# Attention of a two-layer encoder: key bands of 23 and 31 columns in place of 24 and 32, and a new order of half turns, token turns and one score product on TensorE

## The reference, cut to what matters

```
q, k, v = split(rms_norm(x) @ w_in)            # 8 heads of 64, on a 16 x 64 grid
for each query at (row, col):
    row0 = clip(row - 4, 0, 8);  col0 = clip(col - 8, 0, 48)
    keys = grid[row0 : row0+8, col0 : col0+16]                 # 8 x 16 = 128 keys
    p    = softmax(q . k[keys] / 8 + rpb[h, drow, dcol])
    out  = p @ v[keys]
mix = head_rms_norm(concat[out, gmlp(z), fourier(xc)]);   x = x + mix @ w_out
x = x + swiglu(rms_norm(x))
```

## Time and profile before

| | |
|---|---|
| median of 3 runs | 2007.32 us (2007.18 to 2007.69) |
| the profiled execution | 2007.3 us, span 2005.5 us |
| busy: PE, PEld, DVE, ACT, POOL | 99%, 82%, 76%, 45%, 11% of the span |
| granted PE clock | 1.0 (mean 0.999) |
| attention, layer 1 and 2 | about 199 to 290 us and 1190 to 1290 us of the span |
| DMA | 288.91 MB, mean 144 GB/s; 227.77 MB read from and 59.24 MB written to HBM |

### The profile page before, as it was taken

The page is one execution under the profiler, slowest core; times in us unless marked ns, Lnnn a source line. Parts: engine busy times, 40 slices in busy tenths (PEclk is TensorE's granted clock), DMA queues, the critical chain, the costliest instruction groups (busy, mean ns, idle before and its releaser), DMA issues.

```text
span 2005.5 us, 28816 instructions
## 1 busy us (share of the span) xinstructions
PE 1981.8 (99%) x10528; PEld 1647.2 (82%) x10528; DVE 1530.2 (76%) x2511; ACT 895.3 (45%) x1611; POOL 221.0 (11%) x156
## 2 busy tenths in 40 slices
PE   8999999999999999999999999999999999999998
PEld 7887788888888888888898877888888888888887
DVE  8847874799777777787777488567997777778877
ACT  7453873443333333444544549535333333344443
POOL 1221453100000000000013123630000000000000
PEclk9999999999999999999999999999999999999999
DMA  7965743124432338533477668331343233293333
GB/s 247 214 168 154 228 156 119 43 99 170 132 110 90 106 109 288 174 98 96 120 220 193 156 159 245 138 105 58 129 157 118 90 106 110 100 342 99 95 100 122
DMA packets 130988, 288.91 MB, mean 144 GB/s; under 512 B 12960, under 2 KB 17952, under 8 KB 130592
## 3 DMA queue, kind: packets, MB, share of 16 engines
q1 hardware_dynamic: 107584, 241.97, 37.0%
q0 software_dynamic: 10880, 20.97, 6.3%
q10 hardware_dynamic: 12384, 24.12, 3.4%
HBM read 227.77 MB, written 59.24 MB: 143 GB/s over the span
## 4 chain that ended last, share of the span: by engine, by line
PE 89%; DVE 6%; issue 2%; ACT 2%; DMA 0%; DVEq 0%; SPq 0%; ACTq 0%
PE bank L2249 27%; PE bank L2251 27%; PE bank L2250 27%; PE bank L2470 1%; PE bank L2398 1%; PE bank L2547 1%; DVE s_lo L1484 1%; DVE t_lo L1913 0%; PE bank L2492 0%; PE bank L2361 0%; PE bank L2485 0%; ACT logits L1189 0%; PE bank L2377 0%; DVE logits L1772 0%; DVE att_sq L1829 0%
## 5 line engine op out<-in xcount | busy, mean ns | idle before, releaser
L2249 PE MATMUL bank<-t_hi,s_hi 128*128 128x512 f32 (+1 forms) x1336 | 516.9, 387 | 0.8 <-DVE hid_cu L2026 0.5
L2250 PE MATMUL bank<-t_lo,s_hi 128*128 128x512 f32 (+1 forms) x1336 | 516.3, 386 | 0.0
L2251 PE MATMUL bank<-t_hi,s_lo 128*128 128x512 f32 (+1 forms) x1336 | 516.3, 386 | 0.0
L2249 PEld LDWEIGHTS bank<-t_hi,s_hi 128*128 128x128 f32 x1336 | 250.9, 188 | 52.4 <-DVE hid_cu L2026 1.3
L2251 PEld LDWEIGHTS bank<-t_hi,s_lo 128*128 128x128 f32 x1336 | 250.9, 188 | 50.9
L2250 PEld LDWEIGHTS bank<-t_lo,s_hi 128*128 128x128 f32 x1336 | 251.0, 188 | 50.7
L2249 PE MATMUL bank<-b_hi,s_hi 128*128 128x512 f32 x528 | 206.0, 390 | 0.1
L2251 PE MATMUL bank<-b_hi,s_lo 128*128 128x512 f32 x528 | 205.5, 389 | 0.0
L2250 PE MATMUL bank<-b_lo,s_hi 128*128 128x512 f32 x528 | 205.4, 389 | 0.0
L992 ACT ACTIVATE s_hi<-w_u 128x512 fp32r<-128x512 f32 x142 | 89.6, 631 | 233.1 <-PE bank L2251 175.6
L992 ACT ACTIVATE s_hi<-w_down 128x512 fp32r<-128x512 f32 x154 | 97.3, 632 | 201.9 <-PE bank L2251 199.9
(11 more groups left out here) (296 smaller groups left out, 3704.8 us busy)
## 6 DMA issues: line engine op xcount, KB each, us to landing
w_raw<-in_win SPq DMA_DIRECT2D x51, 512.0 KB, 5.8
w_g<-in_wg SPq DMA_DIRECT2D x44, 512.0 KB, 3.6
w_u<-in_wu SPq DMA_DIRECT2D x44, 512.0 KB, 4.5
t_raw<-hidden_t SPq DMA_DIRECT2D x88, 256.0 KB, 2.6
w_raw<-in_win POOLq DMA_DIRECT2D x40, 512.0 KB, 7.1
t_raw<-hidden_b SPq DMA_DIRECT2D x66, 256.0 KB, 2.6
hidden_b<-hid_g SPq DMA_DIRECT2D x60, 256.0 KB, 2.0
hidden_t<-hid_x SPq DMA_DIRECT2D x44, 256.0 KB, 2.0
```

The lines of the kernel that those rows point to most:

```text
L2249: nc.tensor.matmul(bank, lh, rh, start=start, stop=False, skip_group_check=reopened)
L2250: nc.tensor.matmul(bank, lh, rl, start=False, stop=False, skip_group_check=reopened)
L2251: return nc.tensor.matmul(bank, ll, rh, start=False, stop=stop, skip_group_check=reopened)
```

## The change

`KC` becomes 23, 31, 31, 24; a new `KS` keeps 24, 32, 32, 24 for the score products. So scores are computed as before, and the last column of each row of keys in blocks 0 to 2 is dropped when `logits` reads the bank. All that follows uses `KC`: `L`, the bias tables (laid out on the host with fewer columns), the exponentials, the half turns (chunks of 92 or 124 keys), the value band's partitions and the DMAs that fill them. `BAND` stays 0, 8, 24, 40.

In the odd periods 5, 7, 9, 11 and 13 `turn_tokens` is replaced: each of its four turns is cut into two of 64 rows, and these eight, the twelve half turns of turn_halves(2m) and the two first products of scores(2m+2) are put into one interleaved order, in which instructions of array rows 0 to 63 and 64 to 127 mostly alternate. `ot_full` now counts 2 a tile. Period 15 keeps the old form.

```diff
-KC = [24, 32, 32, 24]
+KC = [23, 31, 31, 24]
+KS = [24, 32, 32, 24]
+NTURN = NCHUNK * P
...
         def score_bank(i, e):
-            return B[e + 4 * (i >= SINGLE and i % 2)][:, 0:keys(i // 4)]
+            j, rr = TILES[i // 4]
+            bank = B[e + 4 * (i >= SINGLE and i % 2)]
+            return bank[:, 0:KR[rr] * KS[j]].rearrange("p (r c) -> p r c", c=KS[j])
...
-                sp.wait_ge(ot_full, l * 8 + 8)
+                sp.wait_ge(ot_full, 2 * (l * 8 + 8))
...
-                    act.wait_ge(ot_full, l * 8 + tile + 1)
+                    act.wait_ge(ot_full, 2 * (l * 8 + tile + 1))
...
+                    def by_row(ap):
+                        return ap.rearrange("p (r c) -> p r c", c=KC[TILES[tile][0]])
                     nc.vector.tensor_tensor_reduce(
-                        L[:, t % 4, 0:keys(tile)], score_bank(t // 2, t % 2),
-                        BIAS[BIAS_BUF[tile]][:, h // 4, h % 4 * keys(tile):(h % 4 + 1) * keys(tile)], -1.0, 3e38,
+                        by_row(L[:, t % 4, 0:keys(tile)]), score_bank(t // 2, t % 2)[:, :, 0:KC[TILES[tile][0]]],
+                        by_row(BIAS[BIAS_BUF[tile]][:, h // 4, h % 4 * keys(tile):(h % 4 + 1) * keys(tile)]), -1.0, 3e38,
...
+                def score(i, n, e):
...
+                    mm = nc.tensor.matmul(
+                        score_bank(i, e), qs[hp, c, q0:q0 + P],
+                        grid(ks[hp, c, :])[:, 4 * rr:4 * rr + KR[rr], BAND[j]:BAND[j] + KS[j]],
+                        start=n == 0, stop=n == 2)
...
+                def half_tokens(tile, k, e):
+                    rows = slice(e * DH, (e + 1) * DH)
+                    mm = nc.tensor.transpose(B[TILE_BANK[tile]][:, k * P + e * DH:k * P + (e + 1) * DH],
+                                             head_squares(tile)[rows, k, :], IDENT[rows, rows])
+                    if k == NP - 1:
+                        mm.then_inc(ot_full, 1)
...
+                def turn_halves_and_tokens(i, tile, following):
+                    before = 2 * (l * 8 + tile)
+                    pe.wait_ge(o_norm, l * 8 + tile + 1)
+                    half_tokens(tile, 0, 1)
+                    pe.wait_ge(pt_dve, l * 32 + i)
+                    pe.wait_ge(pt_act, l * 32 + i)
+                    pe.wait_ge(p_made, l * 64 + 2 * i + 1)
+                    for g in range(3):
+                        half_turn(i, g, 0)
+                        half_tokens(tile, g + 1, 1)
+                    pe.wait_ge(p_made, l * 64 + 2 * i + 2)
+                    half_turn(i, 3, 0)
+                    half_turn(i, 0, 1)
+                    half_turn(i, 4, 0)
+                    half_turn(i, 1, 1)
+                    half_turn(i, 5, 0)
+                    half_turn(i, 2, 1)
+                    scores_ready(following)
+                    score(following, 0, 0)
+                    half_turn(i, 3, 1)
+                    half_turn(i, 4, 1)
+                    pe.wait_ge(ot_full, before + 1)
+                    half_tokens(tile, 0, 0)
+                    half_turn(i, 5, 1)
+                    half_tokens(tile, 1, 0)
+                    score(following, 0, 1)
+                    half_tokens(tile, 2, 0)
+                    half_tokens(tile, 3, 0)
...
-                    scores(2 * m)
+                    if m % 2 or m == SINGLE // 2:
+                        scores(2 * m)
+                    else:
+                        score_terms(2 * m, 1)
...
-                    if m % 2:
-                        turn_tokens((m - 5) // 2)
-                    turn_halves(2 * m)
+                    if m % 2 == 0:
+                        turn_halves(2 * m)
+                    elif m < 15:
+                        turn_halves_and_tokens(2 * m, (m - 5) // 2, 2 * m + 2)
+                    else:
+                        turn_tokens(5)
+                        turn_halves(2 * m)
```

More of the change, by code:

```diff
@@ L275, in build @@
         PT = nc.alloc_sbuf_tensor_at("probs_t", [P, 4 * NCHUNK, P], F32, offset=BASE + shared)
-        small[0] = shared + 4 * NKEY * 4
+        small[0] = shared + 4 * NTURN * 4
         for n, name in enumerate(("cu", "u4u", "t4")):
@@ L2393, in scores, with score_terms @@
                         pe.wait_ge(qk_lo, l * 16 + 8 + i + 1)
+                def score(i, n, e):
+                    tile, c = divmod(i, 4)
+                    j, rr = TILES[tile]
                     q0 = (2 * j + rr) * P
-                    for n, (qs, ks) in enumerate(((QH, KH_), (QH, KL), (QL, KH_))):
-                        for e in range(2):
[L2397 to L2403, removed]
+                    hp = slice(DH * e, DH * e + DH)
+                    qs, ks = ((QH, KH_), (QH, KL), (QL, KH_))[n]
+                    mm = nc.tensor.matmul(
+                        score_bank(i, e), qs[hp, c, q0:q0 + P],
+                        grid(ks[hp, c, :])[:, 4 * rr:4 * rr + KR[rr], BAND[j]:BAND[j] + KS[j]],
+                        start=n == 0, stop=n == 2)
+                    if n == 2:
+                        mm.then_inc(s_full, 1)
+                def score_terms(i, first):
+                    for n in range(first, 3):
+                        for e in range(2):
+                            score(i, n, e)
+                def scores(i):
+                    scores_ready(i)
+                    score_terms(i, 0)
                 for k in range(4):
@@ L2475, in values, with heads_ready @@
                                 mm.then_inc(pv_done, 1)
-                def turn_heads(tile):
+                def heads_ready(tile):
                     pe.wait_ge(o_copied, l * 8 + tile + 1)
@@ L2483, in turn_heads @@
                         pe.wait_ge(bt_lo, l * 8 + 8)
+                def turn_heads(tile):
+                    heads_ready(tile)
                     for k in range(NP):
@@ L2540, in turn_halves @@
                     pe.wait_ge(pt_act, l * 32 + i)
[L2541 to L2548, removed]
-                                    L[rows, t % 4, chunk(t // 8, n)], IDENT[rows, rows])
-                                if s == 1 and n == NCHUNK - 1:
-                                    mm.then_inc(pt_full, 1)
+                    for g in range(2 * NCHUNK):
+                        if g % NCHUNK == 0:
+                            pe.wait_ge(p_made, l * 64 + 2 * i + g // NCHUNK + 1)
+                        half_turn(i, g, 0)
+                        half_turn(i, g, 1)
+                def turn_halves_and_tokens(i, tile, following):
[6 more added lines that the diff above has]
+                    for g in range(3):
+                        half_turn(i, g, 0)
+                        half_tokens(tile, g + 1, 1)
[17 more added lines that the diff above has]
+                    half_tokens(tile, 3, 0)
                 last_half_bank(2, (0, 1))
```

22 lines of the change are left out of this document (14 added, 8 removed).

## The result

The kernel after takes **2205.26 us** (median of 4 runs, 2204.11 to 2205.34), the kernel before 2007.39 us (4 runs, 2007.18 to 2007.69): a ratio of 1.0984, 95% interval 1.0967 to 1.1001. The forecast was 2198 us, in a range of 2172 to 2340. The profiled execution took 2205.23 us, span 2203.4, mean granted clock 0.952.

A forecast was written before the change was run, and what follows sets the result against it. PE, busy 99%, bounds the whole program, but in attention a DVE and ACT ring sets a tile's 8.70 us. Sum: 2007.3 - 0.9 (columns) - 0.4 (order) + 185.6 (DMA stalls) + 6 (clock) = 2198 us, range 2172 to 2340.

The forecast's parts named there:

- Item 4: Value band DMAs of 23 or 31 partitions fall to one engine at 24.2 GB/s; six stalls, 185.6 us.
- Equal parts: Dealing rule for DMAs: the largest number of engines up to 16 dividing the partitions; rounding up was the alternative.
- Slow single engine: Rival: a band load moves only 15.0 GB/s an engine whatever its company; 2338 us in all; chance 0.13.
- (a): Stall of values(0) for block 0's band on one engine: 23.1 us, in layer 2 23.7.
- (b): Stall of values(8) for block 1's band, its loads shifted with values(0): 28.5 us a layer.
- (c): Stall of values(16) for block 2's band, queued behind bias halves, w_out and x_res: 40.9 us a layer.
- Item 5: PE's clock at half speed after each of six stalls: 1 us each, 6 us lost, ends 0 and 12.
- Item 3: New order in five odd periods a layer: 0.38 us saved on PE each, only 0.4 us gained in all.
- the ring: Loop setting a tile's 8.70 us: head_norms, logits on DVE, ACT's exponentials to squares, head_sums on DVE; PE waits inside it.
- PE's order decides: Rival: spread loads with PE setting the pace in the odd periods, 0.38 us x 10 gained; 2002.6 us; chance 0.03.
- Item 1: Narrower logits (12 to 13 ns less on DVE) and exponentials (9 to 10 on ACT): 0.9 us gained in both layers.
- Spread loads: Rival: band loads still use many engines, so only small gains remain; 2006.0 us, ends 2002 and 2012; chance 0.10.

The follow-up runs named there:

- e10: Kernel before, value band loads cut into 21 + 3, 25 + 7 and 22 + 10 partitions, block 3 whole: 2031.18 us, ratio 1.0117.
- e1: Kernel after, each value band load issued as two, partitions 0 to 15 and the rest: 2010.46 us, ratio 1.0016 to before.
- e6: Kernel after, loads of 23 and 31 partitions kept, the reload of x issued behind block 2's loads: 2188.76 us, ratio 1.0903 to before.
- e5: Kernel after, block 0's 23-partition loads left whole, those of blocks 1 and 2 cut into 16 + 15: 2057.26 us, ratio 1.0252 to before.
- e3: Kernel before with only the new order of the odd periods, key columns kept at 24, 32, 32, 24: 2008.25 us, ratio 1.0003.
- e9: Kernel before with the new order alone, and the reload of x behind block 2's loads: 2008.82 us, ratio 1.0005.
- e7: Kernel after, band loads cut in two (16 and the rest), reload of x behind block 2's loads: 2007.17 us, ratio 0.9999 to before.
- e4: Dropped columns alone, in the old order of PE, band loads cut into 16 and the rest: 2010.25 us, ratio 1.0013 to before.

## Why the prediction was right

**Item 4, the DMAs.** The two steps that carried the forecast held. Equal parts: one engine at 23 and 31 (share 0.07), seven at 21. The choice itself had less behind it than the prediction says. The row that it names, the missing time to landing, can't part the two ways of dealing: 24 partitions lie on 12 engines by either, and in the trace of before the 24-partition loads leave 13 landing events and the 32-partition loads 16, with both kinds on each semaphore. So from the rows alone the choice was open. The rate: block 0's four loads landed at 207.1, 215.2, 222.5 and 231.0, some 8.0 us for 188,416 bytes, 23.7 GB/s against the 24.2 taken. "Slow single engine" is excluded by the rate. The 15.0 and 11.6 GB/s an engine of the earlier trace rows fit a limit of the sum, and e10 agrees, where seven engines moved 152 to 160 GB/s, some 22 each; the 104 GB/s of e1's small pieces do not fit it and stay unexplained.

The sizes, a layer each (forecast; layer 1, layer 2):

| wait | forecast | measured |
|---|---|---|
| (a) values(0) | 23.1, 23.7 | 23.2, 22.6 |
| (b) values(8) | 28.5, 28.5 | 29.3, 33.0 |
| (c) values(16) | 40.9, 40.9 | 39.35, 39.8 |
| sum of six | 185.6 | 187.2 |

(a) fits to 1.1 us. Of its terms only the 1.65 us to the first data had no row; the trace of after has 1.2 there, and 31.4 us for the four loads instead of 31.1.

(b) and (c) fit partly by luck. A wait for a band ends when the band lands, so the thing to compare is the time from one value product to the next block's landing:

| from, to | forecast | layer 1 | layer 2 |
|---|---|---|---|
| values(0), block 1 landed | 50.3 | 55.0 | 55.9 |
| values(8), block 2 landed | 58.2 | 58.1 | 57.9 |

The first row is the term that the prediction mis-sized, by some 5 us a layer. I had the transfers on the one engine follow each other at a full rate from fixed issue times. In fact SP was held up in its issues: block 1's loads came 6.2 us after values(0) instead of 4.8, and their data came later still, so that they met x_res. While x_res moved (from 274 us on in layer 1), block 1's fourth load took 15.2 and 16.2 us instead of 10 (from the landing before it to its own). In layer 1 the wait was near its forecast even so, only because PE, at the low clock, came to values(8) 4.1 us late itself: one error hid the other. In layer 2 PE was 1.3 us late, and the wait shows the excess.

The second row is right to 0.3 us, but by two errors that cancel: the first of block 2's loads began some 14.3 us after values(8) instead of 16.2, and the fourth took 13.7 instead of 10. (c) is shorter than its forecast because PE came to values(16) 1.6 and 1.0 us late.

e6 shows what x_res adds. Without it ahead, block 2 lands 50.7 and 50.0 us after values(8), which is 7.4 and 7.9 less, and block 1 lands 52.0 and 52.9 us after values(0), 3.0 and 3.1 less. That the wait for block 1 fell by only 0.1 in layer 1 is again PE, which came 2.9 us sooner.

**Item 5, the clock.** The direction was right, the sum was not. Behind the waits the windows show 0.50, half speed, and then a rise. The earlier trace rows gave 3.3 us at half speed. In after it was some 4.5 us behind the third wait (0.50 from 345 to 348, then 0.81 over 4 us, which is 1.5 us more), and some 12.5 us behind the first (0.50 from 231 to 241, then 0.66 over 4 us, 2.7 us more).

What it cost PE, against before: from values(0) to values(8) 25.98 - 21.84 = 4.1 us in layer 1 and 23.15 - 21.84 = 1.3 in layer 2 (waits left out); from (8) to (16) 1.6 and 1.0; from (16) to values(30) 1.4 and 1.0. But only the last pair adds to the time. The others lie ahead of a wait for a band, and shorten it by as much, unless the band's loads start later for them. They do not: block 1's loads were issued 6.2 us after values(0) in both layers, with 4.1 us lost in one and 1.3 in the other, and block 2's before values(8) had started at all (282.57 against 286.45). So the forecast's 6 us should have been some 2.4.

With that the 197.9 us add up: (a) 45.8; values(0) to values(8) 33.4 and 34.3 more than before, where 28.5 each was forecast; values(8) to values(16) 41.0 and 40.8 more; the last restarts 2.4; 197.7 in all. The forecast, 7 us lower, had 10.7 too little for block 1, 3.6 too much for the clock, 1.0 too much for (a), and 1.3 for gains that do not show.

Why the clock stayed low for 12.5 us once is open. In e6, whose code is that of after up to this place, the same wait cost 282.99 - 29.16 - 230.79 - 21.84 = 1.2 us, and in e5 1.3 and 1.1. In these windows the first row is of after, the others of e6:

```profile
236.00:241.00 5.00, 5.00 (x44) 3.75 (x40) 3.41 (x11) 4.87 (x11) 2.55 (x2) 0.50 0.47 145
...
231.00:236.00 5.00, 5.00 (x46) 4.04 (x44) 1.77 (x3) 1.74 (x5) 0.08 (x1) 0.52 0.01 3
236.00:241.00 5.00, 4.50 (x68) 3.44 (x65) 4.18 (x12) 5.00 (x14) 2.49 (x2) 1.00 0.43 146
```

In the 5 us from 231 to 236 PE had been busy 5.00 us in e6 and 4.79 in after, at the same point of the same program. So the 4.1 us are not the price of such a wait, and what delayed the rise that time no run shows.

**Item 3, the order.** On PE the new order does nearly what was forecast. An odd period of after between the waits:

```profile
298.57 0.27 PE L2521 MATMUL bank<-ident,att_sq 64*128 64x64 f32 x1
298.67 0.24 PE L2571 MATMUL bank<-ident,logits 64*124 64x64 f32 x1
...
299.03 0.42 PE L2406 MATMUL bank<-k_hi,q_hi 64*128 64x384 f32 x1
...
299.29 0.40 PE L2521 MATMUL bank<-ident,att_sq 64*128 64x64 f32 x4
299.51 0.42 PE L2406 MATMUL bank<-k_lo,q_hi 64*128 64x384 f32 x2
```

From the first token half to the second pair of score products it is 299.51 - 298.57 = 0.94 us, 0.31 less than the 1.25 of the earlier trace rows (forecast 0.38; e3 shows 0.94 too). Over ten periods that would be 3.1 us. The profiled runs of e3 (layer 1) and e9 show 0.2 us a layer, which is the 0.4 in all that I took; the medians, 2008.25 and 2008.82, do not show it. The saved time comes back where it was forecast, ahead of turn_halves(2m+1). Its first row in before, and in after:

```profile
242.48 0.60 PE L2547 MATMUL bank<-ident,logits 64*128 64x64 f32 x12
```

```profile
300.77 0.58 PE L2571 MATMUL bank<-ident,logits 64*124 64x64 f32 x12
```

From the first token turn to it there are 242.48 - 240.25 = 2.23 us in before and 300.77 - 298.57 = 2.20 in after. What holds it are the copies in the ring, as these rows of DVE and ACT from the same stretch of after suggest:

```profile
297.83 0.69 DVE L1836 SCALAR_TENSOR_TENSOR att_sq<-bank,head_rstd 128x512 f32<-128x512 f32 x1
...
299.01 0.61 ACT L1193 ACTIVATE logits<-logits,minus_max 128x372 f32<-128x372 f32 x1 [0.30 <-DVE minus_max L1779]
...
303.23 0.69 DVE L1803 TENSOR_REDUCE head_ss<-att_sq 128x8 f32<-128x512 f32 x1 [0.40 <-ACT att_sq L1231]
...
306.40 0.69 DVE L1836 SCALAR_TENSOR_TENSOR att_sq<-bank,head_rstd 128x512 f32<-128x512 f32 x1
```

The same two waits as in the earlier trace rows, 0.30 and 0.40 us where there were 0.31 and 0.34, close the ring: DVE waits for ACT's squares and ACT for DVE's logits. A tile takes 306.40 - 297.83 = 8.57 us, forecast 8.6, before 8.70. "PE's order decides" has fallen. The wait for ot_full inside the new order showed no idle time, as taken.

**Item 1, the columns.** Groups by form of after (count | busy us, mean ns), beside the earlier trace rows:

```profile
L1193 ACT ACTIVATE logits<-logits,minus_max 128x372 f32<-128x372 f32 x16 | 9.6, 601 | 1.4 <-DVE minus_max L1779 1.4
...
L1779 DVE CUSTOM_DVE_ANT_0 logits<-bank,bias 128x372 f32<-128x372 f32 x16 | 8.2, 538 | 1.5 <-PE bank L2406 1.5
```

551 to 538 is 13 ns less on DVE (forecast 12 to 13), 608 to 601 is 7 on ACT (9 to 10). Rows of 31 out of 32 cost DVE nothing, so the upper end of 5 us falls away. What became of the 0.9 us for it can't be told within the scatter: layer 1 of e1 is 0.14 us shorter to values(30) than that of e3 (70.62 against 70.76).

**Item 2** stood at nothing. The turns of 92 or 124 keys take the time of 96 or 128: 0.57 to 0.58 us for twelve, before 0.59.

"Spread loads" would have been right for a kernel with its loads cut otherwise: e7, at 2007.17, is that kernel, 1.2 us above the 2006.0 that I gave it.

## What to carry to other kernels

A tile size that is also the partition count of a DMA sets how many engines carry it: ask for the largest number up to 16 that divides it, and beware of primes above 16, for dropping one column of 24 or 32 took the loads from 12 or 16 engines to one and cost 198 us. Where the size must be such a prime, cut the load into 16 and the rest, and check what stands ahead of it on its queue. When you add up stalls, work with landings: a slow stretch that ends in a wait for a DMA only shortens that wait. A reordering is worth what it takes off the ring that sets the pace, here 0.2 us a layer, by two profiled runs, of 1.55 us on PE (five periods of 0.31).

## What the runs showed of the hardware that was not expected

- **A DMA on one engine blocks its issuer.** SP needed 15.56 and 25.10 us to issue four such loads, before 1.57 and 2.10, and what was next in its program waited too.
- **A lone engine slows down in company.** Runs of 2 KB took 84 ns each on the one engine alone, and 125 to 160 ns on average while x_res moved (274 to 286 us). All sixteen engines were busy then, so this one had x_res to move as well; whether that or the memory slows the runs, no run parts.
- **16 + 15 partitions land later than 32.** Block 2's band of layer 2 landed at 1240.6 in e4 and 1240.5 in e1, before at 1236.6; in layer 1 it was 248.2 and 246.9 against 246.6. With x_res behind it (e7) it landed at 238.6 and 1227.6, long before its use.
- **PE stood idle with no releaser.** It did so once in layer 2 of e1 and of e7:

```profile
1239.06 0.69 PE L2409 MATMUL bank<-k_lo,q_hi 64*128 64x384 f32 x2 [2.77 <-issue]
```

```profile
1229.64 0.44 PE L2410 MATMUL bank<-k_hi,q_lo 64*128 64x384 f32 x1 [1.18 <-issue]
```

The first row is of e1, the second of e7; e5 has such a gap of 1.11 us at 1285.88, and e3 that of 0.28 at 1237.22. Each time a 16 KB load of instructions (queue q8) had started 2.5 to 2.7 us earlier (1236.51, 1227.19, 1283.14 and 1234.67) and taken 1.1 to 1.4 us, so that PE went on 1.2 to 1.4 us after its end. In before the load at this place starts at 1234.26 and PE has no such gap. That fits a PE that had run out of instructions, the load having come late; it is only argued, since no run moved these loads. The number of band loads is not the whole cause, since e3 has as many as before. Whether it is also what splits e9's times is open.
